# Layer norm of a four-layer decoder trunk: variance and root as columns of tokens, a weight split moved to GpSimd, leading panels in another order

## The reference

```
def layer_norm(x, g, b):
    xf = x.astype(jnp.float32)
    mu = jnp.mean(xf, axis=-1, keepdims=True)
    var = jnp.mean(jnp.square(xf - mu), axis=-1, keepdims=True)
    return ((xf - mu) * lax.rsqrt(var + LN_EPS) * g + b).astype(x.dtype)
...
        h = layer_norm(DEEPNORM_ALPHA * h + mix, ln1_g[i], ln1_b[i])
        ffn = conv_glu_ffn(h, ffn_w_in[i], ffn_conv_w[i], ffn_conv_b[i], ffn_w_out[i], valid)
        h = layer_norm(DEEPNORM_ALPHA * h + ffn, ln2_g[i], ln2_b[i])
```

## Time and profile before

| | |
|---|---|
| median of three runs | 1401.75 us |
| profiled execution, its own time | 1404.32 us |
| its span (first to last instruction) | 1402.4 us |
| PE busy | 1336.0 us, 95% |
| DVE busy | 945.4 us, 67% |
| ACT busy | 811.3 us, 58% |
| POOL busy | 231.8 us, 17% |
| mean granted TensorE clock | 0.982 of full speed |

### The profile page before, as it was taken

The page is one execution under the profiler, slowest core; times in us unless marked ns, Lnnn a source line. Parts: engine busy times, 40 slices in busy tenths (PEclk is TensorE's granted clock), DMA queues, the critical chain, the costliest instruction groups (busy, mean ns, idle before and its releaser), DMA issues.

```text
span 1402.4 us, 30127 instructions
## 1 busy us (share of the span) xinstructions
PE 1336.0 (95%) x10433; PEld 1267.9 (90%) x10433; DVE 945.4 (67%) x1890; ACT 811.3 (58%) x1637; POOL 231.8 (17%) x216
## 2 busy tenths in 40 slices
PE   7899999999999999999986999999988999999997
PEld 6788999999977999999975899999987888999997
DVE  4665777765797777765685777776564566777754
ACT  5455676654666666654643567665463555766644
POOL 1000034420000044320010003442000000243400
PEclk9999999999999999999988999999998999999999
DMA  7332455556421456566330135655643333366662
GB/s 256 115 107 74 136 172 187 178 179 195 139 76 49 134 180 188 172 189 188 123 100 31 61 121 170 190 178 180 195 124 119 101 97 122 119 186 190 181 214 86
DMA packets 56867, 203.33 MB, mean 145 GB/s; under 512 B 6224, under 2 KB 8272, under 8 KB 56656
## 3 DMA queue, kind: packets, MB, share of 16 engines
q1 hardware_dynamic: 56784, 202.21, 46.1%
HBM read 201.13 MB, written 1.05 MB: 144 GB/s over the span
## 4 chain that ended last, share of the span: by engine, by line
PE 84%; DVE 7%; ACT 6%; issue 2%; DMA 1%; SPq 0%; DVEq 0%; ACTq 0%
PE ps L376 23%; PE ps L380 22%; PE ps L379 22%; PE ps L494 3%; PE ps L395 2%; PE ps L512 2%; PE ps L398 2%; PE ps L399 2%; DVE w_lo L1135 2%; PE ps L477 1%; PE ps L459 1%; ACT w_hi L765 1%; ACT probs L815 1%; DMA cst<-in_consts 1%; PE ps L577 1%
## 5 line engine op out<-in xcount | busy, mean ns | idle before, releaser
L1135 DVE TENSOR_TENSOR w_lo<-raw,w_hi 128x1024 fp32r<-128x1024 f32 x378 | 462.3, 1224 | 254.3 <-ACT w_hi L765 252.6
L376 PE MATMUL ps<-h_hi,w_hi 128*128 128x272 f32 (+1 forms) x1752 | 511.7, 292 | 7.7 <-DVE q_rope L1325 4.9
L765 ACT ACTIVATE w_hi<-raw 128x1024 fp32r<-128x1024 f32 x378 | 396.8, 1051 | 191.7 <-PE ps L376 180.0
L380 PE MATMUL ps<-h_hi,w_lo 128*128 128x272 f32 (+1 forms) x1752 | 504.8, 288 | 0.0
L379 PE MATMUL ps<-h_lo,w_hi 128*128 128x272 f32 (+1 forms) x1752 | 503.6, 287 | 0.0
L376 PEld LDWEIGHTS ps<-h_hi,w_hi 128*128 128x128 f32 x1752 | 330.8, 189 | 15.7 <-issue 5.9
L379 PEld LDWEIGHTS ps<-h_lo,w_hi 128*128 128x128 f32 x1752 | 331.4, 189 | 0.3
L380 PEld LDWEIGHTS ps<-h_hi,w_lo 128*128 128x128 f32 x1752 | 330.9, 189 | 0.0
L376 PE MATMUL ps<-hid_hi,w_hi 128*128 128x272 f32 (+2 forms) x676 | 198.1, 293 | 0.3 <-DVE y L1135 0.2
L379 PE MATMUL ps<-hid_lo,w_hi 128*128 128x272 f32 (+2 forms) x676 | 195.4, 289 | 0.0
L380 PE MATMUL ps<-hid_hi,w_lo 128*128 128x272 f32 (+2 forms) x676 | 195.4, 289 | 0.0
(11 more groups left out here) (153 smaller groups left out, 1751.2 us busy)
## 6 DMA issues: line engine op xcount, KB each, us to landing
raw<-in_weights SPq DMA_DIRECT2D x378, 512.0 KB, 3.7
cst<-in_consts SPq DMA_DIRECT2D x1, 1795.5 KB, 12.3
h<-in_x SPq DMA_DIRECT2D x2, 544.0 KB, 5.5
out<-h SPq DMA_DIRECT2D x8, 128.0 KB, 1.8
```

The source lines that it names most:

```text
L376: m = pe.matmul(b, whi, xhi, start=n == 0, stop=False)
L380: m = pe.matmul(b, wlo, xhi, start=False, stop=n == len(tiles) - 1)
L765: act.activation(w_hi[slot][:], raw[slot][:], ACT.Copy).then_inc(hi_ready, 1)
L1135: return dve.tensor_tensor(out_, a_, b_, op)
```

## The change

- **Column statistics.** Besides `ones` x totals for the mean, PE now takes the totals, the last chunk and its squares as *stationary* operands, in three slices of 128 tokens (0 to 127, 128 to 255, 144 to 271), with one column of `ones` as the moving operand. That gives mean (bank 7) and mean square (bank 4) as three columns with tokens on the partitions: 128x3. Banks 7 and 4 are first written by a product with a matrix of zeros.
- **Variance and root** are then done on 128x3: DVE copies and squares the mean column, subtracts; ACT takes `Sqrt`; DVE the reciprocal. PE spreads it back to 128x272 with the column, broadcast, as stationary operand and the identity as moving operand, into bank 6. `rstd` is now that PSUM bank.
- **Order on PE:** zeros, column sums of the totals, full mean of the totals, wait for the last join, column of the last chunk, column of the last squares, full mean of the last chunk, wait for the reciprocal, spread, then `WARM` = 12 matmuls in place of 28. The full mean square (L523, L527), its square (L863), `Ln` and `Exp` go.
- **Last weight unit:** its low part is written by POOL at the head of `norm`, as soon as its high part and the unit before are ready, and no longer by DVE behind the last join.
- **Centring:** DVE takes chunks 0 and 1 (`CENTER_DVE` = 2), POOL chunks 2 to 7.
- **Leading panels** of the stages that read `h` wait for `h_hi` of a chunk, do w_hi x h_hi and w_lo x h_hi of all leading panels, and only then wait for `h_lo` and do w_hi x h_lo. In the last chunk the order stays by panel. The leading panels of `o` are unchanged.

```diff
-CENTER_DVE = 5
+CENTER_DVE = 2
...
+THIRDS = ((0, P), (P, 2 * P), (T - P, T))
...
-WARM = 28
+WARM = 12
...
-        mean_sq, mean = y[:, 2, :], y[:, 3, :]
+        mean, rstd = y[:, 3, :], ps[:, 6, 0:T]
...
+            def leading_from_h(n, s, u0, p0, count, t0):
+
+                slots = [(u0 + j) % RING for j in range(count)]
+                banks = [bank(p0 + j + s.shift)[:, t0:T] for j in range(count)]
+                for k in range(DC - 1):
+                    at_k = slice(k * P, (k + 1) * P)
+                    pe.wait_ge(norm_hi, 8 * n + k + 1)
+                    for j, (b, slot) in enumerate(zip(banks, slots)):
...
+                        m = pe.matmul(b, w_hi[slot][:, at_k], h_hi[:, k, t0:T], start=k == 0, stop=False)
...
+                        pe.matmul(b, w_lo[slot][:, at_k], h_hi[:, k, t0:T], start=False, stop=False)
+                    pe.wait_ge(h_ready, 8 * n + k + 1)
+                    for b, slot in zip(banks, slots):
+                        pe.matmul(b, w_hi[slot][:, at_k], h_lo[:, k, t0:T], start=False, stop=False)
...
+                for b in (7, 4):
+                    pe.matmul(ps[:, b, 0:3], zero[:], zero[:, 0:3], start=True, stop=False)
+
+                def columns(b, src, last=False):
+
+                    for ch, (lo, hi) in enumerate(THIRDS):
+                        ins = pe.matmul(ps[:, b, ch:ch + 1], src[:, lo:hi], ones[:, 0:1],
+                                        start=False, stop=last and ch == 2)
+                    return ins
+
                 pe.wait_ge(sums_added, 6 * (n + 1))
+                columns(7, totals[:, 0, :])
+                columns(4, totals[:, 1, :])
                 pe.matmul(ps[:, 5, 0:T], ones, totals[:, 0, :], start=True, stop=False)
-                pe.matmul(ps[:, 6, 0:T], ones, totals[:, 1, :], start=True, stop=False)
                 pe.wait_ge(bank_free, p0 + 8)
+                columns(7, h[:, 7, :], last=True).then_inc(mean_col_done, 1)
+                pe.wait_ge(squared, 8 * n + 8)
+                columns(4, squares[:, 1, :], last=True).then_inc(sq_mean_done, 1)
                 pe.matmul(ps[:, 5, 0:T], ones, h[:, 7, :], start=False, stop=True).then_inc(mean_done, 1)
-                pe.wait_ge(squared, 8 * n + 8)
-                pe.matmul(ps[:, 6, 0:T], ones, squares[:, 1, :], start=False, stop=True).then_inc(sq_mean_done, 1)
+                pe.wait_ge(rstd_done, n + 1)
+                for ch, c0 in enumerate((0, 0, P - TAIL)):
+                    lo, hi = ch * P, min(T, (ch + 1) * P)
+                    ins = pe.matmul(ps[:, 6, lo:hi], col[:, 2, ch:ch + 1].broadcast_to([P, P]),
+                                    ident[:, c0:c0 + hi - lo], start=True, stop=True)
+                ins.then_inc(rstd_spread, 1)
...
-                act.activation(eps[:, 2:3], eps[:, 0:1], ACT.Ln)
+                act.activation(eps[:, 2:3], eps[:, 0:1], ACT.Sqrt)
                 square(n, 7)
+                act.wait_ge(var_done, n + 1)
+                act.activation(col[:, 1, :], col[:, 1, :], ACT.Sqrt, bias=eps[:, 0:1]).then_inc(root_done, 1)
                 act.wait_ge(mean_done, n + 1)
-                act.activation(mean_sq, ps[:, 5, 0:T], ACT.Square).then_inc(mean_squared, 1)
                 act.activation(mean, ps[:, 5, 0:T], ACT.Copy).then_inc(mean_copied, 1)
-                act.wait_ge(var_done, n + 1)
-                own.link(act.activation(rstd[:], rstd[:], ACT.Ln, bias=eps[:, 0:1]))
-                act.activation(rstd[:], rstd[:], ACT.Exp, scale=-0.5).then_inc(std_done, 1)
...
             def norm(n, stage):
 
+                st, u0, _ = LAYERS[n // 2][stage]
+                u = u0 + st.units - 1 + AHEAD
+                if u < N_UNITS:
+                    pool.wait_ge(hi_ready, u + 1)
+                    pool.wait_ge(lo_ready, u)
+                    slot = u % RING
+                    pool.tensor_tensor(w_lo[slot][:], raw[slot][:], w_hi[slot][:].bitcast(F32),
+                                       ALU.subtract).then_inc(lo_ready, 1)
                 pool.wait_ge(mean_copied, n + 1)
...
-                        if ending and last_unit[0] < N_UNITS:
-                            split_lo(*last_unit)
...
-                dve.wait_ge(mean_squared, n + 1)
+                dve.wait_ge(mean_col_done, n + 1)
+                own.link(copy(col[:, 2, :], ps[:, 7, 0:3]))
+                own.link(tt(col[:, 0, :], col[:, 2, :], col[:, 2, :], ALU.mult))
                 dve.wait_ge(sq_mean_done, n + 1)
-                tt(rstd[:], ps[:, 6, 0:T], mean_sq, ALU.subtract).then_inc(var_done, 1)
+                tt(col[:, 1, :], ps[:, 4, 0:3], col[:, 0, :], ALU.subtract).then_inc(var_done, 1)
+                dve.wait_ge(root_done, n + 1)
+                dve.reciprocal(col[:, 2, :], col[:, 1, :]).then_inc(rstd_done, 1)
                 dve.wait_ge(mean_copied, n + 1)
                 for k in range(CENTER_DVE):
                     ins = tt(h[:, k, :], h[:, k, :], ps[:, 5, 0:T], ALU.subtract)
                 own.link(ins)
-                dve.wait_ge(std_done, n + 1)
+                dve.wait_ge(rstd_spread, n + 1)
```

More of the change, by code:

```diff
@@ L180 @@
 CONST, N_CONST = const_columns()
-INITS = 8
+INITS = 9
 def build_program(nc, x, weights, consts, out):
@@ L222, in build_program @@
         totals = sb("totals", [P, 2, T])
-        rstd = sb("rstd", [P, T])
+        col = sb("col", [P, 3, 3])
+        zero = sb("zero", [P, P])
         eps = sb("eps", [P, 4])
@@ L245, in build_program @@
         init_done = sem("init_done")
-        mean_done, mean_squared, mean_copied = sem("mean_done"), sem("mean_squared"), sem("mean_copied")
-        sq_mean_done, var_done, std_done = sem("sq_mean_done"), sem("var_done"), sem("std_done")
+        mean_done, mean_col_done, mean_copied = sem("mean_done"), sem("mean_col_done"), sem("mean_copied")
+        sq_mean_done, var_done, root_done = sem("sq_mean_done"), sem("var_done"), sem("root_done")
+        rstd_done, rstd_spread = sem("rstd_done"), sem("rstd_spread")
         sums_added, centered = sem("sums_added"), sem("centered")
@@ L401, in leading_panels @@
                             m.then_inc(panel_done, 1)
+            def leading_from_h(n, s, u0, p0, count, t0):
[5 more added lines that the diff above has]
+                    for j, (b, slot) in enumerate(zip(banks, slots)):
+                        if k == 0:
+                            if p0 + j >= BANKS:
+                                pe.wait_ge(bank_free, p0 if s.shift else p0 + j - (BANKS - 1))
+                            pe.wait_ge(lo_ready, u0 + j + 1)
+                        m = pe.matmul(b, w_hi[slot][:, at_k], h_hi[:, k, t0:T], start=k == 0, stop=False)
+                        if k == 0 and j == 0 and u0:
+                            m.then_inc(w_used, 1)
+                        pe.matmul(b, w_lo[slot][:, at_k], h_hi[:, k, t0:T], start=False, stop=False)
+                    pe.wait_ge(h_ready, 8 * n + k + 1)
+                    for b, slot in zip(banks, slots):
+                        pe.matmul(b, w_hi[slot][:, at_k], h_lo[:, k, t0:T], start=False, stop=False)
+                at_k = slice((DC - 1) * P, DC * P)
+                pe.wait_ge(h_ready, 8 * n + DC)
+                for j, (b, slot) in enumerate(zip(banks, slots)):
+                    m = pe.matmul(b, w_hi[slot][:, at_k], h_hi[:, DC - 1, t0:T], start=False, stop=False)
+                    if j:
+                        m.then_inc(w_used, 1)
+                    pe.matmul(b, w_hi[slot][:, at_k], h_lo[:, DC - 1, t0:T], start=False, stop=False)
+                    pe.matmul(b, w_lo[slot][:, at_k], h_hi[:, DC - 1, t0:T],
+                              start=False, stop=True).then_inc(panel_done, 1)
             def gemm(layer, name, rhs, ready=None, after=None, lead=0, straight=False, led=0):
@@ L409, in turn @@
                         if isinstance(i, int) and i == 0 and j < lead:
-                            if j == 0:
+                            if j == 0 and name in ("o", "down"):
                                 leading_panels(s, u0, p0, rhs, ready, lead, t0, range(led, DC))
+                            elif j == 0:
+                                leading_from_h(2 * layer + (name == "up"), s, u0, p0, lead, t0)
                         else:
@@ L520, in output @@
                 gemm(n // 2, stage, rhs, ready, after, lead=lead, straight=True, led=led)
+                if n == 0:
+                    pe.wait_ge(init_done, INITS)
+                for b in (7, 4):
[5 more added lines that the diff above has]
+                    return ins
                 pe.wait_ge(sums_added, 6 * (n + 1))
+                columns(7, totals[:, 0, :])
+                columns(4, totals[:, 1, :])
                 pe.matmul(ps[:, 5, 0:T], ones, totals[:, 0, :], start=True, stop=False)
-                pe.matmul(ps[:, 6, 0:T], ones, totals[:, 1, :], start=True, stop=False)
                 pe.wait_ge(bank_free, p0 + 8)
+                columns(7, h[:, 7, :], last=True).then_inc(mean_col_done, 1)
```

(12 more changed lines are left out.)

## The result

| | before | after |
|---|---|---|
| median of 4 runs each, us | 1402.17 (1399.26 to 1403.01) | 1430.55 (1429.29 to 1435.88) |
| span of the profiled execution, us | 1402.4 | 1434.1 |
| mean granted clock | 0.982 | 0.967 |

The ratio is 1.0202, 95% interval [1.0177, 1.0227]: the changed kernel is slower by 28.4 us. The forecast was 14.7 us slower; the rival "the clock falls too" said 1434.

A forecast was written before the change was run, and what follows sets the result against it. PE's stream of matmuls was taken as the bound, so only its waits and auxiliary work at the norms could move. Terms 9.6 + 2.0 + 0.6 + 1.2 + 1.3 = 14.7 us on 1401.75 gave 1416, 80% range 1396 to 1438.

The forecast's parts named there:

- the clock falls too: Rival: in the changed norms PE's clock drops to half, 2.5 us a norm, 17.5 in all, 1434 us; chance 0.28.
- What bounds the kernel: PE holds 84% of the chain; only its waits and auxiliary work can move, with 6.45 us between dense stretches per norm.
- Part 3: Last weight split on POOL blocks DVE's last sum: first leading matmul 1.6 us later in six norms, 2.0 in norm 1.
- Parts 1 and 2: Column statistics and small root in each norm: column products 0.11 us each, rescale 0.7 later, leading panels 0.15 later.
- The part by itself is worth nothing: Column statistics and small root, without anything else: leading panels begin 0.15 us later, about 0.2 against it.
- Parts 4 and 5: POOL's centring delays low parts, 1.2 us plus 0.6 in norm 1, and the last norm 1.3; table loads together 0, ±2.6.
- the case without blocking: Rival: POOL's split does not hold up DVE's sum, the other parts cost 5 us, 1407; chance 0.16.
- The sum, without the clock: All norms together: 9.6 + 2.0 + 0.6 + 1.2 + 1.3 = 14.7 us slower, 1416, with no clock fall charged.
- The forecast's likeliest case: POOL's split blocks DVE's last sum in the norms, 14.7 us slower in all, 1416; chance 0.36.
- loads may count as work: Argument against a clock fall in the norms: PE's weight loads with one column moving might keep the clock up; no size.
- PE's idle time: In the changed norm PE idles for its sums before mostly loading weights, named in the clock-fall rival of 17.5 us, chance 0.28.

The follow-up runs named there:

- experiment 4: Kernel before with only the last weight unit's low part moved from DVE to POOL: 1413.80 us, ratio 1.0105 to the kernel before.
- experiment 5: Changed kernel with the last weight split back on DVE and each column product moving 128 columns instead of one: 1402.42 us, ratio 1.0000 to the kernel before.
- experiment 6: Changed kernel, split still on POOL, with each column product moving 128 columns instead of one: 1414.22 us, ratio 1.0077 to the kernel before.
- experiment 1: Changed kernel with the last weight unit's low part written by DVE again: 1411.78 us, ratio 1.0074 to the kernel before.
- experiment 7: Kernel before with a norm's 28 dummy matmuls of 272 moving columns replaced by 56 with two: 1438.38 us, ratio 1.0259.
- experiment 2: Changed kernel plus dense dummy matmuls in PE's waits, 12 before the last sum and 4 before the reciprocal: 1420.46 us, ratio 1.0157 to the kernel before.
- experiment 3: Changed kernel with the last weight split back on DVE and 6 dummies before the reciprocal's wait: 1414.60 us, ratio 1.0096 to the kernel before.

## Why the prediction was wrong

**What bounds the kernel: right.** Everything came out of the stretch of the earlier trace rows.

**Part 3, the split on POOL: right, with its price.** Forecast: POOL 2.65 us, first by about 0.25; measured 2.376, and 0.12 in norm 0 and 0.21 to 0.28 in the others. Forecast: DVE's sum near 3 us, PE's statistics from 159.95 in the old trace, 1.7 behind R; measured 2.67 to 2.84 and 1.54 to 1.91. Forecast: the sum ends 0.58 behind POOL; measured 0.58. Put on the old kernel alone it costs 12.0 us (experiment 4); on the new one with wide columns 1414.22 - 1402.42 = 11.8, or 10.8 by the kernels before beside them. The mutual exclusion that the Trainium skill states (SBUF — State Buffer, section Who interferes with whom) is what the trace shows, 2.84 us where 0.72 had stood.

**Parts 1 and 2: right in the terms that they had.** Column products at 0.11: 1.34 for 12. Rescale at 5.5: 5.49. Leading panels 0.15 later: 6.80 against 6.61, so 0.19. "The part by itself is worth nothing": with the clock held up it is 1.0000 [0.9985, 1.0016] (experiment 5, with parts 4 and 5 in it).

**Parts 4 and 5: right in kind, priced too high.** Low parts 0.4 to 0.5 us longer a norm on DVE, of which 0.2 was charged to the path. The last norm cost 0.67 (12.28 against 11.61 from R to the end), forecast 1.3. With the clock up, all parts but the third came to 0.1 us over the kernel before (experiment 5), where the case without blocking had 5. The tables moved as forecast (20 loads in place of 27; `Exp` loaded in the window mixer at 395.74 and ahead of the forgetting gate at 1089.77, the load of the earlier trace rows in the latent mixer gone); experiment 5 leaves them no visible price.

**The sum, without the clock: right.** Experiment 6 is the forecast's own case, all five parts with the clock up. It took 1414.22; the forecast was 1416. Over the kernel before beside it that is 10.9 us (6.0 to 15.4 by the interval) against 14.7: the terms of part 4 and POOL's 2.65 us were somewhat large, and the times lie closer than the differences because the kernel before was slower in that set of runs.

**The step that failed: the clock was a rival at 0.28 and belonged in the sum.** The forecast's likeliest case charged nothing for it, with "loads may count as work" as the reason. The rival had the mechanism and nearly the price: 17.5 us; the runs say 16.3 to 17.5 (changed kernel against experiment 6; 1.8 to 3.9 a norm at the first leading matmul), or 9.4 with the sum not held up (experiment 1 against 5). That reason is wrong here. Experiments 5 and 7 show it from both sides: the same loads with 128 columns moving kept the clock at full in seven norms of seven, and loads alone, two columns moving and no gap, lost it in seven of seven. The Trainium skill (TensorE: Matmul & The Clock Gate, Part 1: The HAM clock gate) has the clock follow how busy PE was. By the profile's busy column PE had 3.20 of 3.20 us ahead of the fall in experiment 1, so that column is not the measure. The second half of the rival's case, PE's idle time, did nothing alone: idle gaps of 1.4 to 1.7 us in experiment 4 and of 1.1 to 1.4 in experiment 6 cost nothing of the clock. Together with the narrow columns it counted: the time at half clock in the seven norms is 27.3 us without the gap (experiment 1), 64.9 with it, and 13.7 with the gap filled (experiment 2). The profile of before held one hint that I undervalued: the 28 dummies of the earlier trace rows sat just where the new kernel would put its thinnest work.

What stays open: why norms 2 and 4 kept the clock in experiment 1 and the other five did not. Their statistics are the same instructions. Each kernel was traced once, and the mean granted clock of experiment 1's eight runs goes from 0.972 to 0.981, so it may well be other norms, and another number of them, from one execution to the next; no trace here shows it.

## What to carry to other kernels

Where small matmuls replace wide ones, don't ask only what they take but what moves: if a stretch is nearly all loads, widen the moving side, which cost nothing here (12 products: 1.34 us with one column, 1.35 to 1.44 with 128) and kept the clock up; dense matmuls in the gaps around it did so only in part (experiments 2 and 3). Work that starts on GpSimd just ahead of a VectorE instruction that the path waits for was paid nearly in full by that instruction, where both read two SBUF tensors (2.67 to 2.84 us in place of 0.72). And where a rival names a mechanism of the very stretch that the change rebuilds, price it into the sum, not beside it.

## What the runs showed of the hardware

- Weight loads with one or two columns moving did not keep TensorE at 2.4 GHz, though they filled its time: 56 in a row without a gap, and the clock at 0.50 before they were through, in seven norms of seven (experiment 7). The column products of experiment 1 lost it in five of seven, and the same loads with 128 columns moving kept it in seven of seven (experiment 5).
- A product with a 128-wide stationary operand keeps one pace from 1 to 128 moving columns: 0.11 to 0.12 us an instruction (12 in 1.34 us with one column, in 1.35 to 1.44 with 128, both at full clock).
- A 128x1024 subtraction on GpSimd took 2.37 to 2.38 us in seven of seven; a start 0.12 us ahead of VectorE's was enough to hold that one to the end. VectorE's 0.72 us sum then ended 0.58 behind GpSimd in seven of seven.
